# Low parts of the weights in the attention stages: split by GpSimd in place of VectorE

## The chip, the cores and the metric

One core of one Trainium2 chip runs the whole kernel in one launch. The metric is the device time of that launch in microseconds. Engines are named TensorE (PE, with its weight loads PEld), VectorE (DVE), ScalarE (ACT), GpSimd (POOL) and SyncE (SP, which issues most DMAs).

## The reference: what is computed

Two pre-norm residual layers on 512 tokens of width 1024, float32, then a final RMSNorm. In each layer `z = rmsnorm(x) @ w_in` is cut into the inputs of two head groups:

```python
h = rmsnorm(x, g)
z = h @ w_in
u_lru, g_lru, q, g_nsa, kc, vc, ks, vs, kwn, vwn, gate_logits = split(z)
y_lru = rg_lru(causal_depthwise_conv(u_lru, conv_w, conv_b), ...)
o_cmp, p_cmp = cmp_attention(q, compress(kc, ...), compress(vc, ...))
o_slc = slc_attention(q_rot, rope(ks), vs, idx, ok)
o_win = win_attention(q_rot, rope(kwn), vwn)
y_nsa = gates[0] * o_cmp + gates[1] * o_slc + gates[2] * o_win
y = concat([y_lru * silu(g_lru), y_nsa * silu(g_nsa)])
return x + y @ w_out
```

With 512 tokens the selection takes every causal block and the window holds every causal key, so both branches are causal attention with their own keys and values: 8 query heads of width 64, in two groups with one key and value head each.

## The kernel before

**Products in three passes.** Activations and weights lie transposed, 128 rows to a tile. Each operand of a projection is the sum of a rounded high part and a low part, and each 128-row step is three matmuls of 512 columns (`z_piece`, L1603): high by high (L1634), high by the activations' low part (L1635), the weights' low part by high (L1636).

**Weight tiles.** A weight tile is 128 x 1024 float32. SyncE loads it into one of four staging buffers (`stage`, `load` at L754). ScalarE copies it, rounded, into `w_hi` (`split_hi`, L972, activation at L982, semaphore `hi_split`). VectorE subtracts that from the staged tile into `w_lo` (`split_lo`, L1220, subtraction at L1233, semaphore `lo_dve`). `w_hi` and `w_lo` are rings of three tiles (`N_RING`), so the high part of tile n waits until TensorE has used tile n - 3. The last four tiles (`OT`, numbers 58 to 61) go into `h_hi` and `h_lo` instead. Who needs a low part asks through `wait_low` (L674): TensorE before a tile's first matmul, SyncE before it loads into the staging buffer again. There are 62 tiles; the two `gate` tiles are scaled, not split. Only the first two tiles' second halves are subtracted by GpSimd (L945).

**The order of the work.** `schedule()` writes one list of steps by hand; every engine walks through it and does its part of each step. `HI` and `LO` steps (and the `ON` steps, which count as both) mark where ScalarE and VectorE split the next tile. Per layer the list has the projections (`Z`), then `attention(l)` (L129 on), then in layer 0 four `ON` steps and `NORM`. The attention stage begins with `CS2`: VectorE ends the softmax of the compressed branch (sum L1509, reciprocal L1510, gate L1513, row mask L1514), then evicts a projection (`projected`, L1282), and in the second part scales the probabilities (L1506). After that come 12 sets. In each TensorE turns tiles of probabilities (`T`, L1737), fills in with eight or fewer `F` pieces of projections, makes two steps of scores (`S`, L1714 and L1722), and weighs the values (`W`, L1775). VectorE takes the row minima of the scores (`MX`, L1522), ScalarE their exponentials (`EX`, L1160), VectorE the spread coefficients (`K`, L1540 to L1545), which TensorE turns (`T B`, L1747), and the outputs (`O`, L1556 to L1565; `Y`, L1571; `YL`, L1428). `HI` stands ahead of a set's score steps and `LO` behind its `W` steps. In layer 1 the final products `G` (`out_piece`, L1653, matmuls L1668 to L1670) fill in at the end; each of their steps k waits for `OT` tile k's low part.

**GpSimd** sets constants up, and then adds squares in the `ON` steps (L929, L932), takes roots (L940), issues the rope's DMAs (`SWAP`, L963, in the projections), and in the end takes the final norm's roots (L968). In the attention stages it has no step before the first `FMEAN`.

Of the kernel before, what the change touches and what calls it, by code (L numbers as in the profile page):

```python
# [25 lines left out]
F32, F32R, BF16 = mybir.dt.float32, mybir.dt.float32r, mybir.dt.bfloat16  # L26
ALU, ACT, AX = mybir.AluOpType, mybir.ActivationFunctionType, mybir.AxisListType
# [324 lines left out]
class Plan:  # L352


    def __init__(self, sched):
# [64 lines left out]
        for n in range(N_STAGE, len(self.loads)):  # L420
            self.load_at.append(max(self.load_at[-1], ends.get(self.loads[n - N_STAGE], 0)))
        self.load_no = {key: n for n, key in enumerate(self.loads)}
        self.z_no = {key: n for n, (key, *_) in enumerate(self.z)}
        self.aux_no = {key: n for n, (key, *_) in enumerate(self.aux)}
        self.e_no = {key: n for n, key in enumerate(self.e)}
# [72 lines left out]
def hybrid_trunk(nc, x, norm_g, w_in, conv_w, conv_b, lru_wa, lru_ba, lru_wi, lru_bi, lru_lambda,  # L498
                 cmp_pos_k, cmp_pos_v, cmp_k_w1, cmp_k_w2, cmp_v_w1, cmp_v_w2, w_out, final_g,
                 rope_cos, rope_sin, out):  # L500
    sched = schedule()
# [7 lines left out]
    with ctx:  # L509
# [3 lines left out]
        def sem(name):  # L513
            return ctx.enter_context(nc.semaphore(name))
# [67 lines left out]
        stored = sem("stored")  # L582

        first_w, first_hi, lo_pool = sem("first_w"), sem("first_hi"), sem("lo_pool")
        hi_split, lo_dve, cmp_used = sem("hi_split"), sem("lo_dve"), sem("cmp_used")

        z_full, z_dve = sem("z_full"), sem("z_dve")
# [58 lines left out]
        def stage_of(key):  # L646
            return stage[:, load_no[key] % N_STAGE, :]
# [4 lines left out]
        def hi_count(n):  # L652

            return sum(key[2] != "gate" for key in plan.split[:n + 1])

        def split_into(n):

            key, slot = plan.split[n], n % N_RING
            if key[0] == "OT":
                return [h[:, 2 * key[2]:2 * key[2] + 2, :].rearrange("p a n -> p (a n)") for h in (h_hi, h_lo)]  # L660
            return [w_hi[:, slot, :], w_lo[:, slot, :]]
# [11 lines left out]

        def wait_low(eng, n):  # L674

            eng.wait_ge(lo_dve, n + 1)
            if n < 2:
                eng.wait_ge(lo_pool, n + 1)

# [200 lines left out]
        @block.gpsimd  # L880
        def _(pool):
            links = [0]

            def link(ins):

                links[0] += 1
                ins.then_inc(pool_link, 1)
                pool.wait_ge(pool_link, links[0])

            link(pool.memset(ident[:, :], 0.0))  # L890
            link(pool.affine_select(out=ident[:, :], in_=ident[:, :], compare_op=ALU.not_equal, fill=1.0,
                                    base=0, pattern=[[-1, P]], channel_multiplier=1))
            pool.memset(ones[:, :], 1.0).then_inc(first_consts, 1)
            link(pool.memset(ident_b[:, :, :], 0.0))
            for h in range(2):
                rows = slice(h * HD, (h + 1) * HD)
                link(pool.affine_select(out=ident_b[rows, :, :], in_=ident_b[rows, :, :], compare_op=ALU.not_equal, fill=1.0, base=0,
                                        pattern=[[HD, 2], [-1, P]], channel_multiplier=1))
            gate_rows = ident[:, :].rearrange("p (j n) -> p j n", n=GATE_COLS)[:, :, GATE_COLS - N_GATE:GATE_COLS]
            link(pool.tensor_tensor(pick[:, :], gate_rows[:, 0, :], gate_rows[:, 1, :], ALU.add))  # L900
            link(pool.tensor_tensor(pick[:, :], pick[:, :], gate_rows[:, 2, :], ALU.add))
            pool.tensor_tensor(pick[:, :], pick[:, :], gate_rows[:, 3, :], ALU.add).then_inc(consts, 1)
            pool.tensor_tensor(fold[:, :], ident[:, 0:NCOL], ident[:, NCOL:2 * NCOL], ALU.add).then_inc(consts, 1)
            link(pool.memset(causal_b[:, :, :], 0.0))

            for h in range(2):
                rows = slice(h * HD, (h + 1) * HD)
                link(pool.affine_select(out=causal_b[rows, :, :], in_=causal_b[rows, :, :], compare_op=ALU.is_ge, fill=BIG, base=0,
                                        pattern=[[HD, 2], [-1, P]], channel_multiplier=1))
            link(pool.memset(mask_c[:, :, :], 0.0))  # L910

            pool.affine_select(out=mask_c[:, :, :], in_=mask_c[:, :, :], compare_op=ALU.is_ge, fill=BIG,
                               base=-(CMP_LEN - 1), pattern=[[P, TT], [-CMP_STRIDE, NC]],
                               channel_multiplier=1).then_inc(consts, 1)
            link(pool.memset(row_ok[:, :], 1.0))

            pool.affine_select(out=row_ok[:, :], in_=row_ok[:, :], compare_op=ALU.is_ge, fill=0.0,
                               base=-(CMP_LEN - 1), pattern=[[P, TT]], channel_multiplier=1).then_inc(consts, 1)
            pool.memset(kc_bd[:, :], 0.0).then_inc(consts, 1)
            pool.memset(mhalf[:, :], -0.5).then_inc(consts, 1)  # L920
            pool.memset(upad[:, 0:CONV_W - 1], 0.0).then_inc(consts, 1)
            pool.wait_ge(consts, N_CONST)

            def add_square(tag, m):

                n = tag * KT + m
                pool.wait_ge(squared, n + 1)
                if m == 0:
                    pool.tensor_copy(sq_acc, sq_tmp).then_inc(sq_added, 1)  # L929
                else:  # L930
                    pool.wait_ge(sq_added, n)
                    pool.tensor_tensor(sq_acc, sq_acc, sq_tmp, ALU.add).then_inc(sq_added, 1)  # L932

            def root(tag):

                if tag < 0:
                    pool.wait_ge(x_mean, 1)
                else:
                    pool.wait_ge(a_dve, plan.freed(plan.aux, aux_no[("ss", tag)])[1])
                pool.tensor_tensor(rt[:, :], ms[:, :], mhalf[:, :], ALU.pow).then_inc(root_ok, 1)  # L940

            for n in range(2):
                hi, lo = split_into(n)
                pool.wait_ge(hi_split, n + 1)
                pool.tensor_tensor(lo[:, HALF:], stage_of(plan.split[n])[:, HALF:], hi[:, HALF:].bitcast(F32), ALU.subtract).then_inc(lo_pool, 1)  # L945
            root(-1)
            for st in sched:
                kind = st[0]
                if kind == "ON":
                    for m in (2 * st[2], 2 * st[2] + 1):  # L950
                        add_square(st[1], m)
                elif kind == "NORM":
                    root(st[1])
                elif kind == "SWAP":
                    _, l, name = st
                    n = rope_no[(l, name)]
                    pool.wait_ge(z_dve, plan.freed(plan.z, z_no[("Z", l, name)])[1])
                    if n >= N_SWP:
                        pool.wait_ge(rot_ok, n - N_SWP + 1)
                    if name == "ks" and l >= 1:  # L960
                        pool.wait_ge(sq_added, KT * l)
                    for a in range(4):
                        pool.dma_start(swp[32 * a:32 * a + 32, n % N_SWP, :],  # L963
                                       e_slot((l, name))[32 * (a ^ 1):32 * (a ^ 1) + 32, :]).then_inc(swapped[n % N_SWP], 16)
                elif kind == "FMEAN":
                    t = st[2]
                    pool.wait_ge(fin_mean, t + 1)
                    pool.tensor_tensor(fin_rt[:, t:t + 1], fin_ms[:, t:t + 1], mhalf[:, 0:1], ALU.pow).then_inc(fin_root, 1)  # L968
# [230 lines left out]
        def _(dve):  # L1199
# [20 lines left out]
            def split_lo(n):  # L1220

                key = plan.split[n]
                if key[2] == "gate":
                    dve.wait_ge(staged[load_no[key] % N_STAGE], plan.staged_at[key])
                    if key[1] >= 1:
                        dve.wait_ge(z_full, z_no[("Z", key[1] - 1, "gate")] + 1)
                    scale = par[:, PG + KT * key[1]:PG + KT * (key[1] + 1)].rearrange("p (k a) -> p k a", a=1)
                    dve.tensor_tensor(gate_w[:, :, :], gate_part(key), scale.to_broadcast([P, KT, GATE_COLS]),
                                      ALU.mult).then_inc(lo_dve, 1)
                    return  # L1230
                dve.wait_ge(hi_split, hi_count(n))
                hi, lo = split_into(n)
                dve.tensor_tensor(lo, stage_of(plan.split[n]), hi.bitcast(F32), ALU.subtract).then_inc(lo_dve, 1)  # L1233
# [128 lines left out]
            for st in sched:  # L1362
# [10 lines left out]
                if kind == "EV":  # L1373
                    projected(("Z", *st[1:]))
                if kind in ("ON", "LO") and split < len(plan.split):
                    split_lo(split)
                    split += 1
                if kind == "ON" and st[1] + 1 < DEPTH:
                    h_low(st[1], 2 * st[2] + 1)
# [563 lines left out]
```

## Time and profile before

| | |
|---|---|
| median of 3 runs | 543.06 us (539.6, 543.06, 544.32) |
| the profiled execution | 540.08 us |
| its span in the profile | 538.3 us, 8590 instructions |
| granted TensorE clock | 0.999 |
| attention stages | about 142 to 250 us and 401 to 510 us of the span |

The span is what the profile records; the 1.8 us around it belong to the execution's time. All times within the span are counted from its start. "Busy" of an engine counts its instructions, and matmuls of 0.39 us begin every 0.23 us, since they overlap in the pipeline: a busy TensorE says that nothing is missing in its queue, not that it is at its peak. A row of the timeline has start, length, engine, line, operation, what it writes and reads with shapes, and in brackets the idle time in front with what ended it. A row of a line's view has the count, the least, median and greatest length in ns.

### The profile page before, as it was taken

To read this page: it belongs to the slowest core of one execution; us is meant where nothing else is said; L and a number is where in the kernel's file an instruction comes from. 1 tells how busy PE (TensorE), PEld (TensorE's weight loads), DVE (VectorE), ACT (ScalarE), POOL (GpSimd) and SP (SyncE) were. 2 spreads that over 40 slices of the span, in tenths; PEclk is the share of its full clock that TensorE was granted. 3 is DMA by queue.
4 is the path that set the end of the run, shared out by engine and by line. 5 is a ranking of instruction groups with operands and counts; after the bars stand their busy time and mean duration, and the time that the engine had idled before them with its cause. 6 is when DMAs were issued, how large, how long until landed. Compare 5 with 4: busy or idle time off the path is not lost.

```text
span 538.3 us, 8590 instructions
## 1 busy us (share of the span) xinstructions
PE 523.8 (97%) x3095; PEld 395.6 (73%) x3095; DVE 379.9 (71%) x620; ACT 309.9 (58%) x625; POOL 46.8 (9%) x88
## 2 busy tenths in 40 slices
PE   8999999999899999999999999999989999999995
PEld 7777868778677766767887687678777777676784
DVE  3596996679857686855747589668986768678432
ACT  5757735624766666663534772653475656667523
POOL 4101100130000000000520110012100000000000
PEclk9999999999999999999999999999999999999999
DMA  9876464365222222321323845635523232111013
GB/s 263 203 226 185 97 180 103 73 149 126 76 74 65 56 55 69 79 58 40 90 90 98 213 124 142 119 94 119 136 62 96 61 97 52 50 38 34 8 41 117
DMA packets 102426, 54.65 MB, mean 102 GB/s; under 512 B 42080, under 2 KB 100592, under 8 KB 102384
## 3 DMA queue, kind: packets, MB, share of 16 engines
q1 hardware_dynamic: 99232, 49.63, 36.1%
q0 software_dynamic: 1536, 3.15, 2.4%
q10 hardware_dynamic: 1616, 1.32, 0.8%
q8 instruction: 25, 0.41, 0.3%
q14 instruction: 17, 0.14, 0.1%
HBM read 44.12 MB, written 2.10 MB: 86 GB/s over the span
## 4 chain that ended last, share of the span: by engine, by line
PE 67%; DVE 16%; issue 5%; SPq 4%; ACT 3%; DMA 3%; POOL 1%; POOLq 0%; DVEq 0%; ACTq 0%
PE z_ps L1634 10%; PE z_ps L1636 10%; PE z_ps L1635 10%; PE o_ps L1775 5%; PE t_ps L1737 5%; PE a_ps L1775 4%; PE s_ps L1714 3%; DVE w_lo L1233 3%; PE z_ps L1714 3%; PE o_ps L1634 3%; PE o_ps L1636 2%; PE o_ps L1635 2%; ACT probs L1160 2%; DMA swp<-E 2%; DVE E L1282 2%
## 5 line engine op out<-in xcount | busy, mean ns | idle before, releaser
L1634 PE MATMUL z_ps<-h_hi,w_hi 128*128 128x512 f32 x248 | 101.5, 409 | 4.3 <-DVE E L1282 4.2
L1636 PE MATMUL z_ps<-h_hi,w_lo 128*128 128x512 f32 x248 | 97.0, 391 | 0.0
L1635 PE MATMUL z_ps<-h_lo,w_hi 128*128 128x512 f32 x248 | 96.8, 390 | 0.0
L982 ACT ACTIVATE w_hi<-stage 128x1024 fp32r<-128x1024 f32 x54 | 57.1, 1058 | 53.9 <-PE z_ps L1636 29.1
L1233 DVE TENSOR_TENSOR w_lo<-stage,w_hi 128x1024 fp32r<-128x1024 f32 x54 | 65.9, 1220 | 8.6 <-ACT w_hi L982 7.9
L1169 ACT ACTIVATE probsT<-t_ps 128x512 f32<-128x512 f32 (+1 forms) x70 | 41.7, 595 | 43.8 <-PE t_ps L1737 34.1
L1634 PEld LDWEIGHTS z_ps<-h_hi,w_hi 128*128 128x128 f32 x248 | 46.6, 188 | 18.7 <-issue 8.2
L1636 PEld LDWEIGHTS z_ps<-h_hi,w_lo 128*128 128x128 f32 x248 | 46.5, 188 | 10.3
L1635 PEld LDWEIGHTS z_ps<-h_lo,w_hi 128*128 128x128 f32 x248 | 46.7, 188 | 8.3 <-issue 0.2
L1522 DVE TENSOR_REDUCE mn<-s_ps 128x1 f32<-128x384 f32 (+3 forms) x44 | 26.2, 637 | 32.4 <-PE s_ps L1722 32.3
L1160 ACT ACTIVATE probs<-s_ps,mn 128x128 f32<-128x128 f32 (+3 forms) x64 | 33.1, 527 | 16.4 <-DVE mn L1522 16.2
L1634 PE MATMUL o_ps<-h_hi,w_hi 128*128 128x512 f32 x104 | 42.1, 405 | 0.0
L1636 PE MATMUL o_ps<-h_hi,w_lo 128*128 128x512 f32 x104 | 40.6, 390 | 0.0
L1635 PE MATMUL o_ps<-h_lo,w_hi 128*128 128x512 f32 x104 | 40.5, 390 | 0.0
L963 POOL DMA_DIRECT2D swp<-E x48 | 23.8, 502 | 178.1 <-DVE E L1279 104.5
L1737 PEld LDWEIGHTS t_ps<-ident,probs 128*128 128x128 f32 x216 | 25.2, 140 | 12.1 <-issue 6.9
L1737 PE MATMUL t_ps<-ident,probs 128*128 128x128 f32 x216 | 33.5, 278 | 0.0
L1634 PE MATMUL z_ps<-y_hi,w_hi 128*128 128x512 f32 x64 | 27.9, 435 | 0.0
L1775 PE MATMUL o_ps<-probsT,v_sb 128*64 128x256 f32 x208 | 26.6, 386 | 0.0
L1636 PE MATMUL z_ps<-y_hi,w_lo 128*128 128x512 f32 x64 | 25.2, 394 | 0.0
L1635 PE MATMUL z_ps<-y_lo,w_hi 128*128 128x512 f32 x64 | 25.0, 391 | 0.0
L1531 DVE STREAM_TRANSPOSE swp<-probs 128x512 f32<-128x512 f32 x18 | 19.8, 1102 | 6.3 <-DMA probsT<-swp 3.5
(266 smaller groups left out, 1052.7 us busy)
## 6 DMA issues: line engine op xcount, KB each, us to landing
stage<-in_w_in SPq DMA_DIRECT2D x27, 512.0 KB, 4.1
stage<-in_w_in SPq DMA_DIRECT2D x34, 256.0 KB, 3.9
probsT<-swp SPq DMA_DIRECT2D x72, 64.0 KB, 2.1
stage<-in_cmp_k_w SPq DMA_DIRECT2D x8, 512.0 KB, 4.0
stage<-in_cmp_v_w SPq DMA_DIRECT2D x8, 512.0 KB, 4.5
stage<-in_w_out SPq DMA_DIRECT2D x8, 512.0 KB, 3.3
stage<-in_w_out SPq DMA_DIRECT2D x16, 256.0 KB, 3.7
swp<-E POOLq DMA_DIRECT2D x48, 64.0 KB, 2.3
```

The costliest lines, as they stand in the source:

```text
L963: pool.dma_start(swp[32 * a:32 * a + 32, n % N_SWP, :], e_slot((l, name))[32 * (a ^ 1):32 * (a ^ 1) + 32, :]).then_inc(swapped[n % N_SWP], 16)
L982: act.activation(split_into(n)[0], stage_of(key), ACT.Copy).then_inc(hi_split, 1)
L1160: act.activation(probs[:, 4 * pair + 2 * g + r, c0:c0 + W], scored(m, g)[:, at * W:(at + 1) * W], ACT.Exp, scale=-1.0, bias=mn[:, m % 2, g ...
L1169: act.activation(slot_of(key)[0:rows, :], turn_bank(n)[0:rows, :], ACT.Copy).then_inc(pt_act, 1)
L1233: dve.tensor_tensor(lo, stage_of(plan.split[n]), hi.bitcast(F32), ALU.subtract).then_inc(lo_dve, 1)
L1522: dve.tensor_reduce(mn[:, m % 2, g, 0:many], scored(m, g)[:, 0:many * W].rearrange("p (h w) -> p h w", h=many), AX.X, ALU.min).then_inc(mi ...
L1634: pe.matmul(bank, w_hi[:, slot, at:at + P], x_hi, start=first, stop=False)
L1635: pe.matmul(bank, w_hi[:, slot, at:at + P], x_lo, start=False, stop=False)
L1636: ins = pe.matmul(bank, w_lo[:, slot, at:at + P], x_hi, start=False, stop=last)
L1714: pe.matmul(scored(m, g)[:, at * wide:(at + 1) * wide], q_st[rows, GROUP * of_q + q, i * P:(i + 1) * P], keys, start=(at == 0 and part == ...
L1737: ins = pe.transpose(bank[:, j * P:(j + 1) * P], probs[:, 4 * pair + j, c0:c0 + P], ident[:, :])
L1775: ins = pe.matmul(o_bank(l, i, b)[g * HD:(g + 1) * HD, pair * N_PAIR_COL:(pair + 1) * N_PAIR_COL], v, turned, start=first, stop=last, skip ...
```

## The change

In `Plan`, every tile whose low part is due in an attention stage, from `CS2` to the next `ON`, `NORM` or `ZP` step, is given to GpSimd ("pool"), every other one to VectorE ("dve"), each with its count. GpSimd gets a loop step for `ON` and `LO` that waits for the high part and subtracts the whole tile; VectorE passes over those tiles. `wait_low` asks for the semaphore of the engine that made the part. No tile is loaded or rounded elsewhere than before.

```diff
@@ -420,6 +420,17 @@
+        inside, low, counts, n = False, {}, {"pool": 0, "dve": 0}, N_RING
+        for st in sched:
+            inside = st[0] in ("CS2", "LO", "HI") and inside or st[0] == "CS2" or inside and st[0] not in ("ON", "NORM", "ZP")
+            if st[0] in ("ON", "LO") and n < len(self.split):
+                low[n] = "pool" if inside else "dve"
+                n += 1
+        self.low = {}
+        for n in range(len(self.split)):
+            who = low.get(n, "dve")
+            counts[who] += 1
+            self.low[n] = (who, counts[who])
@@ -582,6 +593,7 @@
+        low_pool = sem("low_pool")
@@ -673,7 +685,8 @@
-            eng.wait_ge(lo_dve, n + 1)
+            who, count = plan.low[n]
+            eng.wait_ge(low_pool if who == "pool" else lo_dve, count)
             if n < 2:
                 eng.wait_ge(lo_pool, n + 1)
@@ -944,8 +957,15 @@
             root(-1)
+            split = N_RING
             for st in sched:
                 kind = st[0]
+                if kind in ("ON", "LO") and split < len(plan.split):
+                    if plan.low[split][0] == "pool":
+                        hi, lo = split_into(split)
+                        pool.wait_ge(hi_split, hi_count(split))
+                        pool.tensor_tensor(lo, stage_of(plan.split[split]), hi.bitcast(F32), ALU.subtract).then_inc(low_pool, 1)
+                    split += 1
                 if kind == "ON":
@@ -1373,7 +1393,8 @@
                 if kind in ("ON", "LO") and split < len(plan.split):
-                    split_lo(split)
+                    if plan.low[split][0] == "dve":
+                        split_lo(split)
                     split += 1
```

## Rows read from the trace of the kernel before

**Rows 1.** Page, busy times of the engines: us, share of the span, instructions.

```profile
PE 523.8 (97%) x3095; PEld 395.6 (73%) x3095; DVE 379.9 (71%) x620; ACT 309.9 (58%) x625; POOL 46.8 (9%) x88
```

**Rows 2.** Windows: length, busy PE, PEld, DVE, ACT, POOL, then clock and DMA.

```profile
142.00:250.00 108.00, 105.36 (x759) 75.60 (x758) 76.54 (x129) 67.94 (x160) 0.00 (x0) 1.00 0.25 62
...
401.00:510.00 109.00, 106.88 (x769) 77.20 (x768) 77.05 (x127) 69.55 (x163) 0.00 (x0) 1.00 0.22 56
```

**Rows 3.** Waits of PE in the first attention stage: total us, times, longest.

```profile
PE z_ps L1634 <- DVE E L1282: 2.1, 1, 2.1
PE t_ps L1747 <- DVE probsT L1545: 0.4, 1, 0.4
```

**Rows 4.** Timeline near 235 us, VectorE, ScalarE and TensorE.

```profile
234.02 1.22 DVE L1233 TENSOR_TENSOR w_lo<-stage,w_hi 128x1024 fp32r<-128x1024 f32 x1
...
236.48 0.20 DVE L1540 RECIPROCAL coef<-rs 128x8 f32<-128x8 f32 x1
...
235.96 0.20 ACT L1160 ACTIVATION_READ_ACCUMULATOR probs<-t_ps,mn 128x1 f32 x1
...
237.49 0.63 PE L1747 MATMUL t_ps<-ident,probsT 128*128 128x128 f32 x4 [0.37 <-DVE probsT L1545]
```

**Rows 5.** GpSimd's additions and subtractions, by line: count, shortest/median/longest ns, first and last start.

```profile
L932 POOL TENSOR_TENSOR upad<-upad,swp x7: 1133/1645/1660, 256.3 to 272.6; 128x512 f32<-128x512 f32 x7
...
L903 POOL TENSOR_TENSOR fold<-ident x1: 317/317/317, 4.0 to 4.0; 128x64 f32<-128x64 f32 x1
...
L945 POOL TENSOR_TENSOR w_lo<-stage,w_hi x2: 1287/1399/1511, 10.5 to 15.9; 128x512 fp32r<-128x512 f32 x2
```

**Rows 6.** Timeline near 182 us, ScalarE and VectorE.

```profile
181.19 1.05 ACT L982 ACTIVATE w_hi<-stage 128x1024 fp32r<-128x1024 f32 x1
...
183.71 0.55 DVE L1522 TENSOR_REDUCE mn<-t_ps 128x1 f32<-128x384 f32 x1
```

**Rows 7.** Timeline of an ON step near 256 us, VectorE, GpSimd and ScalarE.

```profile
256.27 0.74 DVE L1217 SCALAR_TENSOR_TENSOR h_lo<-xT,par,h_hi 128x512 fp32r<-128x512 f32 x1
...
259.42 0.69 DVE L1370 TENSOR_TENSOR xT<-xT,z_ps 128x512 f32<-128x512 f32 x1 [0.26 <-PE z_ps L1636]
...
256.32 1.65 POOL L932 TENSOR_TENSOR upad<-upad,swp 128x512 f32<-128x512 f32 x1 [2.36 <-ACT swp L992]
258.97 1.14 POOL L932 TENSOR_TENSOR upad<-upad,swp 128x512 f32<-128x512 f32 x1 [1.01 <-ACT swp L992]
...
258.28 0.61 ACT L992 ACTIVATE swp<-xT 128x512 f32<-128x512 f32 x1
```

**Rows 8.** Timeline where each attention stage begins, ScalarE and VectorE.

```profile
142.56 1.06 ACT L982 ACTIVATE w_hi<-stage 128x1024 fp32r<-128x1024 f32 x1 [0.22 <-PE z_ps L1636]
...
143.71 0.21 DVE L1513 TENSOR_TENSOR rsc<-rsc,gates 128x32 f32<-128x32 f32 x1
143.95 0.19 DVE L1514 TENSOR_TENSOR rsc<-rsc,row_ok 128x32 f32<-128x32 f32 x1
144.18 0.69 DVE L1282 TENSOR_TENSOR E<-z_ps,rstd 128x512 f32<-128x512 f32 x1
...
401.89 1.06 ACT L982 ACTIVATE w_hi<-stage 128x1024 fp32r<-128x1024 f32 x1 [0.21 <-PE z_ps L1636]
...
403.04 0.21 DVE L1513 TENSOR_TENSOR rsc<-rsc,gates 128x32 f32<-128x32 f32 x1
```

**Rows 9.** Timeline of the last two weight tiles, ScalarE, VectorE and TensorE.

```profile
501.55 2.00 ACT L982 ACTIVATE h_hi<-stage 128x1024 fp32r<-128x1024 f32 x2
...
502.63 2.36 DVE L1233 TENSOR_TENSOR h_lo<-stage,h_hi 128x1024 fp32r<-128x1024 f32 x2 [1.32 <-ACT h_hi L982]
...
505.51 0.48 PE L1668 MATMUL z_ps<-h_hi,q_st 128*128 128x512 f32 x1
...
506.65 0.48 PE L1668 MATMUL z_ps<-h_hi,q_st 128*128 128x512 f32 x1
```

**Rows 10.** Chain that ended last, behind these tiles: start, us, what.

```profile
508.04 1.88 PE a_ps L1775 x16
```

## The prediction

> **What bounds the kernel now.** I read the page's busy times first: TensorE is busy 97% of the span, VectorE 71%, ScalarE 58% and GpSimd 9% [rows 1]. The change touches only the two attention stages, so I read next the stretches 142 to 250 us and 401 to 510 us: TensorE is busy 105.4 of 108 and 106.9 of 109 us, VectorE about 77 us, GpSimd not at all [rows 2]. Nearly nothing is to be had from a lighter VectorE unless TensorE waits for it. The waits of TensorE in the first stretch say how much it does: 2.1 us once, for the eviction at L1282, and 0.4 us once, for the spread coefficients at L1545 [rows 3]; the second stretch has the 2.1 us wait again and no other of these. So in 217 us of attention, VectorE costs TensorE 4.6 us, in three places. All that matters is whether a removed or an added instruction stands before one of the three, or makes a fourth.
>
> **What the change removes.** I went through the plan with the diff's rule: tiles 22 to 29 (layer 0: gn3, OL 0 to 3, ON 0 to 2) and 53 to 61 (layer 1: gn3, OL 0 to 3, OT 0 to 3) move, 17 in all; everything from the first ON step to the next CS2 stays. VectorE loses 17 x 1.22 us [rows 4] = 20.7 us. Of the three waits, the 2.1 us ones end at 145.01 and 404.35, and the first moved subtraction runs behind them (146.61, 405.95), so its removal gives them nothing. The third does have one in front: the subtraction at 234.02 delays L1564, L1565 and the coefficients, whose chain starts at 236.48 and ends in TensorE's start at 237.49 instead of about 236.9 [rows 4]. Without it that chain can start once the exponential's sum is read, 235.96 + 0.20 = 236.16, so at 236.2: gain 236.48 - 236.2 = 0.3 us. In layer 1 the same chain already waits for ScalarE and gains nothing.
>
> **What it adds.** The price of a 128x1024 subtraction on GpSimd is in no row. The nearest are 128x512 additions there, 1133 ns at the least, a 128x64 one at 317 ns, and two 128x512 subtractions of this very kind at 1399 ns on average [rows 5]. The slope from 64 to 512 elements is (1133 - 317)/448 = 1.82 ns, so 1133 + 512 x 1.82 = 2.07 us; doubling 1133 gives 2.27; doubling 1399 gives 2.8, though the longer ones overlap VectorE work. I take 2.25 us and keep 2.07 to 2.8. That is 38 us on an idle engine, and GpSimd has nothing queued behind it in attention but, much later, the root steps L968.
>
> GpSimd starts right behind ScalarE's high part, while VectorE's subtraction stood behind the row minima. For 13 of the 17 tiles this is harmless: the tile whose high part runs from 181.19 is typical. GpSimd would run from 182.3 to 184.6 beside row minima and an eviction that take one operand from PSUM [rows 6], and TensorE reads that tile only after the two in the ring ahead of it, 24 matmuls each, more than 10 us on. Such one-operand work is not slowed by GpSimd: the addition into xT at 259.42 took 0.69 us, its usual time, with a GpSimd addition running since 258.97 [rows 7]. So I cost the 13 at nothing. At 438 and 454, in layer 1, GpSimd's end may touch the small L1543 of the coefficients; that holds VectorE some 0.2 us, and TensorE waits for no coefficients in that layer. If that cover were gone too, it would be 0.2 us each.
>
> Two places are not harmless.
>
> **The start of attention (tiles 22 and 53).** The high part ends at 142.56 + 1.06 = 143.62; GpSimd follows ScalarE by 0.08 us (258.28 + 0.61 to 258.97) [rows 7], so it starts at 143.70. At that instant VectorE is in the chain L1513 (143.71), L1514 (143.95), L1282 (144.18), and TensorE waits for L1282 [rows 8]. L1513 and L1514 are tiny, but both their operands lie in SBUF. What happens between such a pair of instructions? One direction is shown: where a two-operand VectorE instruction began just before a GpSimd addition (256.27 before 256.32), GpSimd took 1.65 us; where it was nearly over, 1.14 us [rows 7]. The difference, 0.5 us, is about the body of the 0.74 us VectorE instruction, so GpSimd stood still for all of it, and VectorE lost nothing. The other direction, VectorE arriving second, is in no row. Its cost lies between 0 (VectorE has precedence) and GpSimd's whole instruction. A way that is taken by one at a time, for an instruction, fits the row best, and I take the whole: VectorE's chain, 0.5 us from its end, is held until GpSimd is done. If GpSimd wins at 143.70 it ends at 145.95, and L1282 starts at 146.42 instead of 144.18: +2.24 us. If L1513 wins, GpSimd enters at its end, 143.92, before L1514 and the delay is 2.2 to 2.4. Layer 1 has the same spacing: 401.89 + 1.06 = 402.95 against 403.04 [rows 8]. TensorE, already idle, idles 2.2 us longer, twice: +4.5 us, bounds 0 and 2 x 2.9 = 5.8.
>
> The Trainium skill ("SBUF — State Buffer", section Who interferes with whom) states this as a rule: a VectorE instruction with two SBUF inputs shares an exclusive read interface with a GpSimd instruction that reads SBUF, and whichever issues second stands fully blocked. The trace before shows it for GpSimd second and not for VectorE second; by the rule the term is +4.5, without it 0.
>
> **The last two tiles (60 and 61).** Their high parts run from 501.55 to 503.55. VectorE now takes the low parts at once, 502.63 to about 505.0, and TensorE needs the second at 506.65 [rows 9]. GpSimd takes 502.63 to 504.9 and 504.9 to 507.15; TensorE needs the first at 505.51 and gets it, and the second comes at 507.25 instead: +0.6 us (0.2 at 2.07 us each, 1.7 at 2.8). Behind it the chain that ends the span is TensorE's own, matmul after matmul [rows 10], so nothing gives it back. Tile 29, the other one without many steps between, starts on GpSimd about 249.3 and ends by 251.6; the two ON tiles ahead of it keep TensorE busy for 48 matmuls from 248.26, past 259.
>
> **The sum** against the profiled execution (540.08 us, span 538.3): -0.3 + 4.5 + 0.6 = +4.8, so 544.9. The median of the runs shown is 543.06, 3 us above that execution, and the difference goes onto it: 547.9 us. The earlier staging releases only make SyncE's loads earlier; VectorE's 20.7 us are won where it waits anyway.
>
> **The rivals.**
> - *VectorE is never held* (chance 0.30). For it: every VectorE row beside a GpSimd one keeps its usual length. Against: in all of them VectorE came first or had one SBUF operand. The sum is -0.3 + 0.6 = +0.3: 543.4 us.
> - *Contention everywhere* (0.10). GpSimd's subtraction is nearer 2.8 us: 2 x 2.8 + 1.7 - 0.3 = +7.0, so 550.1. For it: the two rows of this very subtraction, 1.29 and 1.51 us. Against: the 1.13 us additions, and that the longer of the two stood beside a VectorE subtraction.
> - *VectorE's relief reaches TensorE* (0.05), the one that ends below. If the 20.7 us freed let the evictions at 144.18 and 403.51 and the coefficients come before TensorE wants them, all three waits go: -4.6, so 538.5 us. It decides on whether anything removed stands ahead of 144.18; in the plan nothing does, and the subtraction at 140.96 (tile 21) stays.
> - The change does what it says: the two semaphores count separately, and each waiting engine asks for the right one. No chance is kept for this.
>
> **Numbers.** The forecast has 0.55. My range is 541.0 to 550.5: it takes in the rival without holding and the dear GpSimd, and the spread of the three runs, 4.7 us, makes it no narrower. Measured against about 1%, which is what a measurement of this kernel can tell from no change: +4.8 us is 0.9%, so a good part of the forecast's case and all of the dear one lie above 548.5. Slower 0.29, within 1% 0.65, faster 0.06.
>
> **What would show it.** GpSimd: 17 subtractions of 2.1 to 2.4 us, busy 46.8 + 38 = about 85 us; VectorE's L1233 x41. The wait of TensorE for L1282 at the start of each attention: 4.3 us for right, 2.1 for the first rival. A new wait of TensorE of some 0.6 us at L1668 or its weights near 511. The wait for L1545 nearly gone. I am wrong if L1513 and L1514 keep their places behind L1510, or if GpSimd's subtraction takes over 3 us.

## The result, and the profile after

| | before | after |
|---|---|---|
| median of the runs | 543.35 us (539.6 to 544.32, 4 runs) | 550.06 us (549.4 to 550.91, 4 runs) |
| the profiled execution | 540.08 us | 550.91 us |
| its span | 538.3 us | 548.8 us |
| mean granted clock of TensorE | 0.999 | 0.985 |

The ratio is 1.0159 (95% interval 1.0129 to 1.0188): slower by 1.6%. The time lies inside my range, but I had given "within 1%" the greatest chance (0.65) and "slower" 0.29, and forecast +4.8 us where the medians show +6.7 and the two profiled executions +10.8. Two executions of the experiments below, one of before at 864.46 us and one of evict_first_after at 1324.49 us, were in the slow state and are left out of every ratio and range.

The page of after, its busy times (they answer to [rows 1]):

```profile
PE 529.7 (97%) x3095; PEld 400.8 (73%) x3095; DVE 366.9 (67%) x603; ACT 310.3 (57%) x625; POOL 87.3 (16%) x105
```

The work moved as the diff says: 17 instructions less on VectorE, 17 more on GpSimd. GpSimd is busy 87.3 us; I had said about 85. Its new groups, by line (they answer to [rows 5]):

```profile
L967 POOL TENSOR_TENSOR w_lo<-stage,w_hi x13: 2335/2362/2390, 144.1 to 462.2; 128x1024 fp32r<-128x1024 f32 x13
L967 POOL TENSOR_TENSOR h_lo<-stage,h_hi x4: 2364/2370/2388, 478.4 to 514.6; 128x1024 fp32r<-128x1024 f32 x4
```

A whole tile takes 2.36 us, where I took 2.25, and all 17 lie within 55 ns of each other (2335 to 2390). Then what TensorE waited for, over the whole span (it answers to [rows 3]):

```profile
PE z_ps L1655 <- DVE E L1302: 8.6, 2, 4.3
...
PE z_ps L1689 <- POOL h_lo L967: 0.6, 1, 0.6
```

The lines have moved by 20 or 21 (L1655 was L1634, L1302 was L1282, L1534 and L1535 were L1513 and L1514). The reader is to see that both 2.1 us waits have become 4.3 us, that the last tile has a wait of 0.6 us, and that the 0.4 us wait for the coefficients is gone from the list. These waits are the prediction's to a tenth. Now the instant at which each attention stage begins, on the timeline of after: VectorE, then GpSimd, then ScalarE's high part (they answer to [rows 8]):

```profile
144.13 2.38 DVE L1534 TENSOR_TENSOR rsc<-rsc,gates 128x32 f32<-128x32 f32 x1
146.54 0.19 DVE L1535 TENSOR_TENSOR rsc<-rsc,row_ok 128x32 f32<-128x32 f32 x1
146.77 0.69 DVE L1302 TENSOR_TENSOR E<-z_ps,rstd 128x512 f32<-128x512 f32 x1
...
144.11 2.33 POOL L967 TENSOR_TENSOR w_lo<-stage,w_hi 128x1024 fp32r<-128x1024 f32 x1 [21.85 <-ACT w_hi L1002]
...
142.97 1.06 ACT L1002 ACTIVATE w_hi<-stage 128x1024 fp32r<-128x1024 f32 x1 [0.21 <-PE z_ps L1657]
...
408.17 2.38 DVE L1534 TENSOR_TENSOR rsc<-rsc,gates 128x32 f32<-128x32 f32 x1
...
408.15 2.34 POOL L967 TENSOR_TENSOR w_lo<-stage,w_hi 128x1024 fp32r<-128x1024 f32 x1 [22.04 <-ACT w_hi L1002]
```

GpSimd starts 0.08 us behind the high part and 0.02 us ahead of the gate's multiplication. That one, 32 elements wide and 0.21 us before, now takes 2.38 us: a held instruction is shown as a long one, since VectorE has begun it, and no list of waits names GpSimd.

If the waits were all, the span would be 538.3 + 2 x 2.2 + 0.6 - 0.3 = 543.0. It is 548.8. Where the rest sits can be seen from windows around and behind the first wait in after (length, then busy PE, PEld, DVE, ACT and POOL, then the granted clock):

```profile
142.00:147.30 5.30, 1.31 (x8) 0.87 (x6) 5.16 (x6) 1.82 (x3) 2.33 (x1) 0.96 0.29 99
147.30:154.10 6.80, 6.49 (x21) 5.15 (x21) 2.67 (x6) 1.71 (x3) 0.00 (x0) 0.53 0.25 77
154.10:160.00 5.90, 5.90 (x45) 4.32 (x44) 0.85 (x2) 2.74 (x4) 0.36 (x1) 1.00 0.00 0
```

The same place in before, behind the 2.1 us wait:

```profile
145.00:152.00 7.00, 6.99 (x37) 5.76 (x38) 3.54 (x6) 2.82 (x5) 0.00 (x0) 1.00 0.25 76
```

In after, TensorE did 21 matmuls and transposes in 6.8 us, in before 37 in 7.0. The granted clock is 0.50, which is 1.2 GHz in place of 2.4, from 146.9 to 153.7, for 6.8 us; the first 0.7 us of them lie in the wait itself. In the second stage it is 0.50 from 409.7 to 416.6. On the timeline of TensorE in after, the matmuls of one product stand 0.43 us apart there, and 0.23 us once the clock is back:

```profile
147.61 0.77 PE L1655 MATMUL z_ps<-h_hi,w_hi 128*128 128x512 f32 x1 [4.29 <-DVE E L1302]
148.17 0.63 PE L1656 MATMUL z_ps<-h_lo,w_hi 128*128 128x512 f32 x1
148.60 0.63 PE L1657 MATMUL z_ps<-h_hi,w_lo 128*128 128x512 f32 x1
...
154.40 0.39 PE L1656 MATMUL z_ps<-h_lo,w_hi 128*128 128x512 f32 x1
154.63 0.40 PE L1657 MATMUL z_ps<-h_hi,w_lo 128*128 128x512 f32 x1
```

Setting the same instructions of both traces side by side tells where the 10.5 us arise. The table gives how far after is behind before:

| instruction | before | after | behind | added |
|---|---|---|---|---|
| last turn ahead of the first wait | 142.30 | 142.71 | 0.41 | 0.4, ahead of any change |
| first matmul behind it | 145.01 | 147.61 | 2.60 | 2.2 |
| last turn ahead of the second wait | 401.63 | 406.75 | 5.12 | 2.5: half clock 2.8, less the coefficients' gain 0.3 |
| first matmul behind it | 404.35 | 411.65 | 7.30 | 2.2 |
| first matmul of the last tile | 506.65 | 517.13 | 10.48 | 3.2: half clock 2.3, last tile 0.9 |

After that row nothing changes until the end. So 4.4 us are the two holds, 5.1 us the clock behind them (the lag grows from 2.6 to 5.4 us behind the first wait, and from 7.3 to 9.6 behind the second), 0.9 the last tile and 0.4 older than any change; 0.3 is gained at the coefficients, as forecast. The last tile costs more than its listed wait of 0.65 us: its first matmul starts 2.03 us behind that of the tile ahead (515.10 to 517.13), and 1.14 us in before (505.51 to 506.65).

### The profile page after: what moved, and what is told of

The parts are those of the page before. It is cut to its first block, busy times and chain, and to the rows that moved or that the text cites. A ratio compares the mean times of both kernels' runs of the same rounds, so it can differ in the third digit from the quotient of the medians.

```text
span 548.8 us, 8590 instructions
## 1 busy us (share of the span) xinstructions
PE 529.7 (97%) x3095; PEld 400.8 (73%) x3095; DVE 366.9 (67%) x603; ACT 310.3 (57%) x625; POOL 87.3 (16%) x105
## 4 chain that ended last, share of the span: by engine, by line
PE 67%; DVE 16%; issue 5%; SPq 4%; ACT 3%; DMA 3%; POOL 2%; POOLq 0%; DVEq 0%; ACTq 0%
PE z_ps L1655 11%; PE z_ps L1657 10%; PE z_ps L1656 10%; PE o_ps L1796 5%; PE t_ps L1758 5%; PE a_ps L1796 3%; PE s_ps L1735 3%; DVE w_lo L1253 3%; PE z_ps L1735 3%; PE o_ps L1655 2%; PE o_ps L1657 2%; PE o_ps L1656 2%; DMA swp<-E 2%; ACT probs L1180 2%; DVE E L1302 2%
## 5 line engine op out<-in xcount | busy, mean ns | idle before, releaser
L1655 PE MATMUL z_ps<-h_hi,w_hi 128*128 128x512 f32 x248 | 103.6, 418 | 8.6 <-DVE E L1302 8.6
L1657 PE MATMUL z_ps<-h_hi,w_lo 128*128 128x512 f32 x248 | 98.6, 398 | 0.0
L1656 PE MATMUL z_ps<-h_lo,w_hi 128*128 128x512 f32 x248 | 98.6, 397 | 0.0
L1655 PEld LDWEIGHTS z_ps<-h_hi,w_hi 128*128 128x128 f32 x248 | 47.8, 193 | 22.5 <-issue 11.9
L967 POOL TENSOR_TENSOR w_lo<-stage,w_hi 128x1024 fp32r<-128x1024 f32 x13 | 30.7, 2361 | 182.4 <-ACT w_hi L1002 182.4
L1657 PEld LDWEIGHTS z_ps<-h_hi,w_lo 128*128 128x128 f32 x248 | 47.7, 192 | 10.7
L1253 DVE TENSOR_TENSOR w_lo<-stage,w_hi 128x1024 fp32r<-128x1024 f32 x41 | 50.1, 1222 | 6.9 <-ACT w_hi L1002 6.1
L1543 DVE TENSOR_REDUCE mn<-s_ps 128x1 f32<-128x384 f32 (+3 forms) x44 | 26.2, 638 | 42.4 <-PE s_ps L1743 42.3
L1656 PEld LDWEIGHTS z_ps<-h_lo,w_hi 128*128 128x128 f32 x248 | 47.9, 193 | 8.7 <-issue 0.2
L1655 PE MATMUL o_ps<-h_hi,w_hi 128*128 128x512 f32 x104 | 42.1, 405 | 0.0
L1655 PE MATMUL z_ps<-y_hi,w_hi 128*128 128x512 f32 x64 | 27.9, 435 | 0.0
```

The lines of the kernel that those rows point to most:

```text
L967: pool.tensor_tensor(lo, stage_of(plan.split[split]), hi.bitcast(F32), ALU.subtract).then_inc(low_pool, 1)
L1543: dve.tensor_reduce(mn[:, m % 2, g, 0:many], scored(m, g)[:, 0:many * W].rearrange("p (h w) -> p h w", h=many), AX.X, ALU.min).then_inc(mi ...
L1655: pe.matmul(bank, w_hi[:, slot, at:at + P], x_hi, start=first, stop=False)
L1656: pe.matmul(bank, w_hi[:, slot, at:at + P], x_lo, start=False, stop=False)
L1657: ins = pe.matmul(bank, w_lo[:, slot, at:at + P], x_hi, start=False, stop=last)
```

## The experiments

Theory A is the hold, TensorE's longer idle time, and the clock that falls behind it. Its rivals are named where they are told apart. In the edits, "pool" marks a tile for GpSimd. Each ratio is against the kernel before in runs on the same chip; the number behind "clock" is TensorE's mean granted clock.

**keep_first: the two first tiles back on VectorE.**

```diff
-                low[n] = "pool" if inside else "dve"
+                low[n] = "pool" if inside and n not in (22, 53) else "dve"
```

> The changed kernel with the first moved tile of each attention stage (22 and 53) given back to VectorE; the other 15 stay on GpSimd. Theory A (GpSimd's subtraction of those two tiles holds VectorE's short two-operand chain, TensorE idles 4.3 us, and its granted clock then falls to half for some 6.8 us): both waits are 2.1 us again, no half-clock stretch, span about 538.3 - 0.3 + 0.6 = 538.6 us, ratio to the kernel before 0.997 to 1.002. Theory B (the loss is spread, each of the 17 subtractions on GpSimd slows its neighbours a little): 15/17 of the 10.5 us of span stay, so about 547.6 us, ratio 1.014.

Measured: ratio 1.0013 (0.999 to 1.0036), span 541.5 us at clock 0.991; its ten runs go from 540.35 us at clock 0.998 to 544.33 us at 0.991. The waits are 2.1 us again:

```profile
PE z_ps L1655 <- DVE E L1302: 4.2, 2, 2.1
...
PE z_ps L1689 <- POOL h_lo L967: 0.6, 1, 0.6
```

Fifteen of 17 tiles on GpSimd cost at most 0.36%, or 2 us, and nothing that stands clear of noise, so theory B with its 1.014 falls. But the profiled span missed 538.6 by 2.9 us, and half clock has come up here too, 3.4 us of it behind each wait of 2.1 us: a window from 145.0 to 148.5 has a granted clock of 0.69.

**only_first: those two tiles alone on GpSimd.**

```diff
+                low[n] = "pool" if inside and n in (22, 53) else "dve"
```

> The kernel before with tiles 22 and 53 alone on GpSimd. Theory A: nearly the whole loss, 2 x 2.2 us of hold and 2 x 3.2 us of half clock, span about 549 us, ratio 1.013 to 1.020. Theory B: 2/17 of 10.5 us, span about 539.5 us, ratio 1.002.

Measured: ratio 1.0097 (1.006 to 1.0135), span 546.4 us, waits 8.3 us in two; clock 0.986 to 0.993 over the runs. Two tiles of 17 carry the greater part of the loss. The interval only just reaches theory A's lower end, 1.013, and the profiled span misses its 549 us by 2.6: behind the first wait half clock lasts 6.8 us as in after, behind the second 3.4.

**fill_after: the change, with TensorE busy in the wait.** The transposes go to a PSUM bank that nobody uses then: TensorE first waits until the exponentials have read it. No result changes.

```diff
+                    if st[1][0] == "Z" and st[1][2] == "gn1" and st[2] == 0:
+                        pe.wait_ge(exp_ok, plan.exps[per_layer(plan.steps, st[1][1]) + 2])
+                        for _ in range(40):
+                            pe.transpose(s_ps[0][:, 0:P], ident[:, :], ident[:, :])
                     z_piece(st[1], st[2])
```

> The changed kernel, and TensorE makes 40 transposes of the identity into an idle PSUM bank just before it waits for the held eviction, so that it isn't idle for 4.3 us; GpSimd and VectorE are as in the change. Theory A: the hold stays (L1513's counterpart still takes 2.4 us), the half-clock stretches go, the mean granted clock is 0.998 or more, and the span is 538.3 + 4.4 + 0.3 = 543 us, some 6 us under the changed kernel's 548.8; ratio to the kernel before about 1.00 to 1.009. Theory C (the clock falls for another reason than TensorE's wait, or costs nothing): span stays at 548 to 549 us.

Measured: ratio 1.0052 (1.0034 to 1.007), span 541.8 us, clock 0.997 to 0.999 in all ten runs. GpSimd and VectorE, on its timeline:

```profile
143.13 0.21 DVE L1534 TENSOR_TENSOR rsc<-rsc,gates 128x32 f32<-128x32 f32 x1
143.38 2.25 DVE L1535 TENSOR_TENSOR rsc<-rsc,row_ok 128x32 f32<-128x32 f32 x1
145.66 0.69 DVE L1302 TENSOR_TENSOR E<-z_ps,rstd 128x512 f32<-128x512 f32 x1
...
143.15 2.43 POOL L967 TENSOR_TENSOR w_lo<-stage,w_hi 128x1024 fp32r<-128x1024 f32 x1 [21.84 <-ACT w_hi L1002]
```

Here VectorE's first short instruction came 0.02 us ahead of GpSimd and kept its 0.21 us; the next one was held. It is the second of the two cases that the prediction had worked out: the eviction starts 2.53 us behind L1534 where it is 0.47 us in before, a delay of 2.1 us. The hold is there and the half clock isn't (only the span's end has any), and the span is 7.0 us shorter than after's. It is 1.2 us under the 543 us expected: TensorE was 0.5 us ahead of before's trace already when attention began, and gained 0.7 near 340 us at a wait for ScalarE, neither of which the edit touches. Theory C falls: the clock fell because TensorE stood idle, and useless matmuls keep it up.

**delay_2 and delay_1: the same wait without GpSimd.** The kernel before, with two additions (or one) of 1024 elements in VectorE's chain ahead of the gate's multiplication; their result is used by nobody.

```diff
+                    for _ in range(2):
+                        link(dve.tensor_tensor(swp[:, :, :].rearrange("p a (b n) -> p (a b) n", n=P), ones_wide, ones_wide, ALU.add))
```

> The kernel before, nothing on GpSimd in attention, with two additional VectorE additions of 1024 elements (about 2.4 us together) in the chain before L1513. Theory A (the length of TensorE's wait decides, whoever causes it): waits of 4.5 us, half clock behind each, span 538.3 + 2 x 2.4 + 2 x 3.2 = 549.5 us. Theory D (it is GpSimd's traffic that costs beyond the wait): only the two waits, 538.3 + 4.8 = 543 us, clock 0.998.

> The kernel before with one addition of 1024 elements (1.2 us) in VectorE's chain, none of it on GpSimd: waits of 3.3 us in place of 2.1 and of the 4.6 us that two additions gave. If each wait is followed by one half-clock stretch of 3.4 us in every execution, as behind 4.6 us, span is 538.3 + 2.4 + 3.4 = 544.1 us less some tenths, clock 0.991 to 0.992 in all runs; if the clock falls only in some executions, as behind 2.1 us, the runs spread from 540.7 to 544.

Measured for two: ratio 1.01 (1.0069 to 1.0132), span 545.7 us, all four runs within 0.1 us, clock 0.991 to 0.992. For one: 1.0073 (1.0048 to 1.0099), span 544.1 us, clock 0.991 to 0.992 in all four. Their waits, first of two additions, then of one:

```profile
PE z_ps L1637 <- DVE E L1283: 9.2, 2, 4.6
```

```profile
PE z_ps L1637 <- DVE E L1283: 6.8, 2, 3.4
```

A wait without any of GpSimd's work in it is followed by half clock too, so theory D's 543 us falls. But theory A's 549.5 us for two additions misses too. Half clock lasted 3.4 us at each wait and not 6.8 us as in after, and cost 1.4 us each. With one addition the sum came out: 544.1 us expected and 544.1 in the profiled execution (543.0 to 544.8 over the four), with 3.4 us of half clock at each wait. So the length of the wait does not decide how long the clock stays down: 4.6 us gave 3.4, 4.3 us gave 6.8.

**fill_before: the kernel before, with TensorE busy in its 2.1 us wait** (the edit of fill_after with 20 transposes).

> The kernel before with 20 transposes of the identity on TensorE in its 2.1 us wait. Runs of the kernel before come with a clock of 0.991 to 0.999, and the lower the clock the longer the time. Theory A (the spread of the kernel before is the clock falling behind these waits): clock 0.998 or more in every run and span 538 to 539 in every run, so a ratio of 0.995 to 0.999. If the spread has another cause, the runs lie between 538 and 542 us of span as before.

Measured: ratio 0.9957 (0.9938 to 0.9976), span 538.0 us, six runs from 538.97 to 539.94 us at clock 0.997 or 0.998. The clock is below the 0.998 expected in two of the six, and no span is above 538.2. The 17 executions of the kernel before that were run beside the last group of kernels go by their clock: 539.66 to 540.78 us at 0.998 or 0.999, 540.54 to 542.19 at 0.995 or 0.996, 542.34 to 543.43 at 0.991 or 0.992. So half clock already followed its 2.1 us waits in many executions, behind none, one or both of them, and the execution whose profile I had read (540.08 us, clock 0.999) was one where it did not. That these steps are whole stretches is read from the traces of keep_first, only_last and pool_later, since no slower execution of before itself has a trace.

**pool_later: GpSimd takes the two tiles a little later.**

```diff
                         pool.wait_ge(hi_split, hi_count(split))
+                        if split in (22, 53):
+                            pool.wait_ge(cs_ok, st[1] + 1)
```

> The changed kernel; GpSimd subtracts tiles 22 and 53 only once VectorE has scaled the compressed probabilities (two more waits, all 17 tiles stay on GpSimd). Theory A (what costs is the instant at which GpSimd takes the way): TensorE's waits are 2.1 us again, as with the two tiles on VectorE; span 538.6 to 541.5 us by the clock, ratio 0.999 to 1.004. Theory B (those two tiles are late, or GpSimd's load as such costs): 548 us.

Measured: ratio 1.0023 (1.0009 to 1.0037), span 539.7 us, clock 0.991 to 0.995. All 17 tiles are on GpSimd and the waits are 2.1 us each, so neither load nor lateness costs; the instant does. The hold moved on, to the coefficients, which nobody awaits yet:

```profile
145.84 0.68 DVE L1407 SCALAR_TENSOR_TENSOR silu_g<-silu_g,E 128x512 f32<-128x512 f32 x1
...
146.67 2.13 DVE L1566 TENSOR_TENSOR coef<-coef,gates 128x8 f32<-128x8 f32 x1
...
146.07 2.70 POOL L969 TENSOR_TENSOR w_lo<-stage,w_hi 128x1024 fp32r<-128x1024 f32 x1 [24.39 <-DVE cmpb L1529]
```

GpSimd's 2.70 us is itself 0.34 longer than the usual 2.36: a two-operand VectorE instruction (L1407), begun 0.23 us earlier, was ahead of it.

**only_last: the last two tiles alone on GpSimd** (`n in (60, 61)`).

> The kernel before with the last two tiles (60 and 61) alone on GpSimd. The term of the sum says a wait of 0.6 us for h_lo and nothing else: profile beside one of the kernel before with the same clock +0.6 to +0.7 us of span (538.9 at a clock of 0.998, about 542 at 0.991), ratio 1.000 to 1.002. If the two tiles cost more, the ratio is 1.003 or above.

Measured: ratio 1.0018 (1.0 to 1.0036), span 542.3 us at clock 0.991, with the one new wait:

```profile
PE z_ps L1689 <- POOL h_lo L967: 0.7, 1, 0.7
```

That fits the term, but the interval doesn't shut out 1.003. As in after, the first matmul of the last tile starts 2.04 us behind that of the tile ahead, where it is 1.14 us in before, so the price is 0.9 us.

**evict_first: the eviction ahead of the softmax.** One swap of two steps in `attention(l)`, on three kernels: before, after, and after with tiles 60 and 61 back on VectorE.

```diff
-    add(("CS2", 0))
     close()
+    add(("CS2", 0))
```

> The kernel before, with the eviction of gn0 put ahead of the compressed softmax's sum instead of behind its first part, in both layers. Theory A (TensorE's 2.1 us wait at the start of each attention stage is the softmax chain in front of that eviction, and in some executions the clock falls behind it): the wait shrinks to some 0.5 us, no half-clock stretch in any run (clock 0.998 or more), span 538.3 - 2 x 1.6 = 535 us in every run, ratio to the kernel before 0.985 to 0.992. Rival (the wait moves on to the next user of the softmax): the span stays at 538 or more.

> The changed kernel with the same reordering. Theory A: GpSimd still holds VectorE's gate multiplication for some 2 us, but TensorE no longer waits behind it, so nearly all of the loss goes: span 535 - 0.3 + 0.6 = 535.4 us, ratio to the kernel before 0.986 to 0.993. Theory B (contention of the 17 subtractions in general): about 535 + 5 to 10 us.

> The changed kernel with the eviction ahead of the softmax's sum, and the last two tiles (60 and 61) back on VectorE; 15 tiles on GpSimd. Theory A: the 0.6 us wait for h_lo goes, so does the 0.4 us wait for the coefficients; span 535.3 - 0.6 = 534.7 us, 0.2 us under the reordered kernel without GpSimd (534.9), ratio to the kernel before 0.990. If GpSimd's remaining 15 tiles cost anything, it is above 535.3.

Measured:

| kernel | ratio to before | span | clock |
|---|---|---|---|
| evict_first_before | 0.9906 (0.9892 to 0.992) | 534.9 us | 0.997 to 0.998 |
| evict_first_after | 0.9916 (0.9901 to 0.9931) | 535.3 us | 0.997 to 0.999 |
| evict_first_not_last | 0.9901 (0.988 to 0.9922) | 535.1 us | 0.997 to 0.999 |

From the timeline of evict_first_after, VectorE and then GpSimd:

```profile
142.66 0.69 DVE L1302 TENSOR_TENSOR E<-z_ps,rstd 128x512 f32<-128x512 f32 x1 [0.30 <-PE z_ps L1657]
...
144.99 1.33 DVE L1534 TENSOR_TENSOR rsc<-rsc,gates 128x32 f32<-128x32 f32 x1
...
143.86 2.39 POOL L967 TENSOR_TENSOR w_lo<-stage,w_hi 128x1024 fp32r<-128x1024 f32 x1 [21.83 <-ACT w_hi L1002]
```

GpSimd still holds VectorE, here for 1.1 us, and nobody waits behind it: TensorE's wait is 0.4 us in each layer. With the order mended, 17 tiles on GpSimd or none makes a difference of 0.4 us of span, about what the last tile costs (0.9 us) less what the coefficients gain (0.3 us). With 15 tiles on GpSimd the span is 535.1 us where 534.7 was expected, so a cost of some tenths is not excluded. The three kernels overlap in their intervals. All beat both kernels of the study: the kernel before by 0.9%, the changed one by about 2.5% (1.0159 over 0.9906). The change itself adds nothing to that.

**How long half clock lasts, over all these traces.** In windows of the granted clock, each stretch at 0.50 has a beginning and a length. TensorE's two waits have one column each:

| trace | length of the waits | half clock begins, first wait | second wait | it lasts |
|---|---|---|---|---|
| after | 4.3, 4.3 | 0.7 us before the wait ends | 1.9 before | 6.8, 6.8 |
| only_first | 4.1, 4.1 | 1.1 before | 1.1 behind | 6.8, 3.4 |
| delay_2 | 4.6, 4.6 | 0.5 before | 0.3 before | 3.4, 3.4 |
| delay_1 | 3.4, 3.4 | 0.1 before | 0.6 behind | 3.4, 3.4 |
| keep_first | 2.1, 2.1 | 1.2 behind | 0.7 behind | 3.4, 3.4 |
| only_last | 2.1, 2.1 | 1.4 behind | 0.5 behind | 3.4, 3.4 |
| pool_later | 2.1, 2.1 | none | 0.4 behind | 3.4 |
| before | 2.1, 2.1 | none | none | |

From the windows of only_first, the end of its first wait and then the short stretch behind its second:

```profile
145.72:146.78 1.06, 0.01 (x1) 0.04 (x1) 0.99 (x3) 0.12 (x1) 0.13 (x1) 0.50 0.00 0
...
411.96:415.38 3.42, 3.42 (x12) 2.72 (x11) 1.25 (x4) 0.60 (x1) 0.00 (x0) 0.50 0.30 104
```

The three stretches of 6.8 us are the three that had begun 0.7 us or more before TensorE had work again; the ten that began later all lasted 3.4. only_first has both, with GpSimd's subtraction in both waits, so the subtraction alone doesn't make the long one. No run set the beginning on purpose, so this is an order seen in 13 stretches, and not shown as the cause.

## Why the prediction was right or wrong

- **What bounds the kernel, what is removed.** Right. VectorE's 20.7 us were worth nothing in general; the wait for the coefficients, 0.4 us, is gone from the list, and the gain is the 0.3 us forecast (its "about 236.9" for TensorE's earliest start is misread: the row's idle time of 0.37 us before 237.49 begins at 237.12). The rival by which VectorE's relief reaches TensorE fell.
- **GpSimd's price.** 2.36 us against my 2.25. The two halves' mean, doubled, gave 2.8 and was the worse guide: beside the longer of the two, a VectorE subtraction ran for its first 0.35 us.
- **The start of attention, the hold.** Right in mechanism, place and size: L1513's counterpart took 2.38 us, and the waits grew by 2.2 us each. No row of before had shown the case in which VectorE arrives second; the runs show that it is then held until GpSimd's instruction ends (2.38 us in after, 1.33 in evict_first_after, 2.13 in pool_later). The rival without a hold fell. The rule of the Trainium skill ("SBUF — State Buffer", section Who interferes with whom) is borne out in both directions: GpSimd second took 2.70 us in pool_later in place of 2.36.
- **The last tiles.** Right in kind, 0.6 us forecast: the listed wait is 0.65 us in after and 0.7 alone, but TensorE starts 0.9 us later in both.
- **The 13 harmless tiles.** Right as far as TensorE goes: keep_first. Of the two places where VectorE's L1543 might be touched, one was: its counterpart at 464.15 takes 0.42 us in place of 0.17, and TensorE loses nothing by it.
- **The step that failed is the sum.** "TensorE, already idle, idles 2.2 us longer, twice: +4.5 us" charged an idle TensorE with its idle time alone, and put what the wait does to the clock at nothing without a reason. At each longer wait the clock fell to half for 6.8 us, which cost 2.8 and 2.3 us more in the profiled executions, 5.1 us in all. fill_after takes that away and leaves the hold; delay_2 and delay_1 bring a shorter stretch about without GpSimd. The Trainium skill ("TensorE: Matmul & The Clock Gate", section Part 1: The HAM clock gate) says that the array's clock follows how busy it has lately been, and the runs agree (fill_after: 0.997 to 0.999 with TensorE kept busy, after: 0.985 to 0.988); I had looked at the granted clock of 0.999 in before as a fact of the kernel, not as one that hangs on its waits.
- **The second error: the yardstick.** I put 3 us between the profiled execution and the median down to nothing in particular and carried them over. The later runs of before, 2 to 3 us longer at a clock of 0.991 than at 0.999, say that they were the half clock of before itself; the clock of those first runs is not on record. That accounts for most of why the medians differ by 6.7 us and the profiles by 10.8: before already paid a part in most of its runs.
- The rival "contention everywhere" named 550.1 us, next to the measured 550.06. It was not right for that: its 2.8 us per subtraction was 2.36, and no contention that costs TensorE anything is there beyond the two instructions at the start of attention.

What stays open is what makes half clock last 6.8 us at the waits of after and 3.4 us at the longer ones of delay_2. The traces put it beside the instant at which the clock falls: 0.7 to 1.9 us before TensorE has work again for the long ones, 0.5 us before or later for the short ones. Why the clock falls when it does, between 1.9 us before and 1.4 us behind the end of a wait, no run shows.

## What to carry to other kernels

Before work goes to GpSimd, look for the instant at which it will start, and for what VectorE does then: a VectorE instruction with two operands in SBUF, of 32 elements a row as much as a large one, can be held until GpSimd's ends (0.21 us became 2.38), and it matters only if TensorE waits behind it. Price a wait of TensorE of some us at more than its length, since half clock can follow (here 1.4 to 2.8 us for each), and look at the clock of several runs before a profile is taken as the kernel's time. The cheapest gain was neither engine's load but the order: what TensorE waits for comes first in VectorE's queue.

## What had not been expected of the hardware

A wait of 2.1 us was followed by half clock in some executions and not in others (0.991 to 0.999 for the kernel before), one of 3.4 or 4.6 us in all eight of delay_1 and delay_2. The trace of pool_later has both: full clock behind its first wait of 2.1 us, 3.4 us of half clock behind its second. The spread of this kernel's times is mostly that: beside fill_before 18 executions of the kernel before ran from 540.47 to 543.88 us, and six with TensorE kept busy in two places from 538.97 to 539.94, a spread of 1.0 us in place of 3.4.
